# Two-block transformer kernel: the squares of three RMS norms are summed by narrower ones-products, placed later in their weight slot

## The chip, the cores and the metric

The kernel runs on one core of a Trainium2 chip. The metric is the device time in microseconds (us) of one execution; for the kernel before it is the median of three runs.

## The reference, cut to what matters

The input x has 256 tokens and 1024 features. Two "hybrid" layers (conv, mLSTM, gated linear attention, sparse attention) come first, then one block of the form

```python
h = h + 0.5 * swiglu(rmsnorm_2(h, ffn1_norm), ...)     # feed-forward part 1
n = rmsnorm_2(h, mix_norm)                             # the mixer
h = h + merged(attention(n @ w_in), gmlp(n @ w_in), gates(n)) @ w_out
h = h + 0.5 * swiglu(rmsnorm_2(h, ffn2_norm), ...)     # feed-forward part 2
return rmsnorm_2(h, final_norm)
```

where `rmsnorm(x, g) = x * rsqrt(mean(x*x, axis=-1) + 1e-6) * g`, the mean going over the 1024 features of one token. Everything is in float32.

## The kernel before, in words

**Layout.** Activations are kept transposed: `x` is 128 partitions by 8 feature tiles (`KT`) by 256 tokens (`T`). So the sum of squares over the features of a token is a sum over 8 tiles and then over 128 partitions, and the second sum is a product with a matrix of ones on TensorE.

**Weights.** They stream through the kernel as "slots" of 128 x 1024 floats. SyncE fetches slot after slot into a ring of five buffers (`raw`); ScalarE writes each slot's rounded high part into `ring` (`split`, L538), GpSimd in two halves (L415), or VectorE for some slots (L1073), writes the remainder as the low part. A slot is multiplied in 24 TensorE instructions: for each of 8 feature tiles, high weight by high x, low weight by high x, high weight by low x (`PARTS`, `tile_product`, L1803).

**The norm at the start of a part.** The norm's factor is per token, so it can be applied to the product instead of to x. The parts start with the gain applied to x (`early`, L555, and `early_lo`, L1083), multiply at once, and multiply the result by the factor when it is evacuated. The factor comes about like this. ScalarE squares x in four pieces of two tiles (`squares`, L544; the first goes to PSUM bank 3). VectorE adds the four pieces in three additions of 512 columns (`add_squares`, L1090), so that two tiles of 256 tokens side by side are left in `sqs[:, 0:512]`. TensorE multiplies each of the two with the 128 x 128 ones and accumulates both into `ps[4][:, 0:256]` (`sum_squares`, L1790). These two products have operands of plain float32 and show as four passes in the trace. VectorE scales to a mean (L1066), ScalarE takes the inverse root as exp(-0.5 ln) (L516, L517), VectorE refines it once (L1102 to L1106) and the factor is ready in `rms`.

**Where it stands in TensorE's order.** `first_two` (L1852) multiplies the part's first two slots, 48 instructions. Then `around_squares` (L1810) does the third slot: 12 instructions for the feature tiles 0 to 3, the sum of the squares, 12 instructions for the tiles 4 to 7. The part's fourth slot follows. After it TensorE needs PSUM banks again that the first slots filled: in a feed-forward part it waits for `ffn_t` (L2272), which VectorE sets when it has multiplied the first gate's result with the factor (L1542); in the mixer it waits in `m_bank_free(4)` (L2354) for `early`, set by VectorE's `early_result(0)` (two instructions of L1693).

**The five calls.** `around_squares(bank, slot, n)` is called with n = 0 and 1 for the two hybrid layers, 2 for feed-forward part 1 (starting near 586 us), 3 for the mixer (767 us), 4 for feed-forward part 2 (926 us). The final norm uses code of its own.

**Orders written out by hand.** Each engine's list is fixed in the source. Around the change VectorE's is: `early_lo`, `add_squares`, then for n = 4 the split of a weight slot (`split(FFN2_AT - 1)`, L1742, recorded at L1073), then `factor`. For n = 2 and n = 3 `factor` follows at once. ScalarE's is: `early`, `squares`, two weight splits (one for n = 4), the load of a function table (L511), a weight split, `factor`. A `step(...)` on VectorE makes the engine wait for the end of its own instruction before the next.

Of the kernel before, what the change touches and what calls it, by code (L numbers as in the profile page):

```python
# [24 lines left out]
ALU = mybir.AluOpType  # L25
# [3 lines left out]
P = 128  # L29
D = 1024  # L30
T = 256
KT = D // P
LAYERS = 2
# [106 lines left out]
GELU_A, GELU_B = 0.044715, 0.7978845608028654  # L140
N_UPDATES = 4
FINAL = LAYERS + 3
FINAL_AT = (LAYERS + 1) * (KT // 2)


# [14 lines left out]
def build(nc, d, out):  # L160
    ctx = ExitStack()
    with ctx:
# [3 lines left out]
        def sem(name):  # L166
            return ctx.enter_context(nc.semaphore(name))
# [50 lines left out]
        sqs = y[:, 8:16, :].rearrange("p a t -> p (a t)")  # L218
# [17 lines left out]
        def branch(k, part):  # L236

            return ys[:, k, part, :] if k < 4 else xs[:, k - 4, part, :]
# [18 lines left out]
        ps = [ctx.enter_context(nc.psum_tensor(f"ps{b}", [P, 512], F32)) for b in range(8)]  # L257
# [15 lines left out]
        ones = const[:, C_ONE:C_ONE + P]  # L273
# [11 lines left out]
        S = {n: sem(n) for n in names}  # L285
# [27 lines left out]
        def _(sp):  # L313
# [72 lines left out]
            for k in (0, 2, 6, 4):  # L386
                if k == 6:
                    sp.wait_ge(S["last_f"], 1)
                else:
                    sp.wait_ge(S["x_f"], FINAL_AT + k // 2 + 1)  # L390
                sp.dma_start(out[:, k:k + 2, :], xn[:, k:k + 2, :]).then_inc(S["stored"], 16)
# [660 lines left out]
        def _(dve):  # L1052
            step = Steps(dve, S["dve_steps"])
            tt, ts, stt = dve.tensor_tensor, dve.tensor_scalar, dve.scalar_tensor_tensor
# [10 lines left out]
            def mean_square(dst, src, n, done):  # L1065
                ts(dst, src, 1.0 / n, EPS, ALU.mult, ALU.add).then_inc(done, 1)  # L1066
# [19 lines left out]
            def add_squares(n):  # L1086

                for b in range(1, 4):
                    dve.wait_ge(S["sq"], n * 4 + b + 1)
                    ins = tt(ps[3][:, :] if b < 3 else sqs[:, 0:512], ps[3][:, :], sqs[:, b * 512:(b + 1) * 512],  # L1090
                             ALU.add)
                    if b < 3:
                        step(ins)
                ins.then_inc(S["sq_sum"], 1)

            def factor(n, copy=False):
# [58 lines left out]
            early_lo(0, par, V_G, True, range(4, KT))  # L1155
            split(-RING + 1)
            add_squares(0)
            split(-RING + 3)
            dve.wait_ge(S["const_in"], 16)
            dve.wait_ge(S["par_in"], 16)  # L1160

            for it in range(LAYERS):
# [315 lines left out]
                first = {50: [(ml_denominator, 2)], 52: [(ml_denominator, 3)], 65: [(ml_pair, 1)]}  # L1478
# [53 lines left out]
                update_x(it, it * LAYER_SLOTS + LAYER_SLOTS, 1.0)  # L1532
                early_lo(it + 1, par, V_G)
                add_squares(it + 1)
                split(base + LAYER_SLOTS - 1)


            def ffn(at, n, h_done, y_done, last):
# [55 lines left out]
                if not last:  # L1594
                    update_x(n, at + FFN_SLOTS, 0.25)
                    early_lo(n + 1, par2, U_MIX)
                    add_squares(n + 1)
                    for p in range(at + FFN_SLOTS - 2, at + FFN_SLOTS):
                        split(p)
# [145 lines left out]
            def end_update(a, b):  # L1745

                dve.wait_ge(S["end_out"], a // 2 + 1)
                dst = flat(x[:, a:b, :])
                stt(dst, ps[4 + a // 2][:, a % 2 * T:a % 2 * T + (b - a) * T], 0.25, dst, ALU.mult, ALU.add)\
                    .then_inc(S["end_x"], 1)  # L1750
# [14 lines left out]
            end_update(7, 8)  # L1765
            dve.wait_ge(S["ssq"], FINAL + 1)
            mean_square(var[:, 0:2], ps[4][:, 0:2], D, S["end_var"])
# [12 lines left out]
        def _(pe):  # L1780
            mm = pe.matmul

            def sum_squares(n):

                if n == 0:
                    pe.wait_ge(S["bias_sb"], 1)
                    pe.wait_ge(S["const_in"], 16)
                pe.wait_ge(S["sq_sum"], n + 1)
                for c in range(2):
                    last = mm(ps[4][:, 0:T], ones, sqs[:, c * T:(c + 1) * T], start=(c == 0), stop=(c == 1))  # L1790
                last.then_inc(S["ssq"], 1)

            PARTS = ((0, 0), (1, 0), (0, 1))
# [1 line left out]
            def tile_product(bank, half, slot, rhs, ks=range(KT), at=0, ready=None, freed=False, first=True, final=True):  # L1795

                order = [(k, w, x) for k in ks for w, x in PARTS]
                if ready:
                    order = [(k, w, 0) for k in ks for w in (0, 1)] + [(k, 0, 1) for k in ks]
                for i, (k, wp, xp) in enumerate(order):  # L1800
                    if ready and wp == 0:
                        ready(k, xp)
                    last = mm(ps[bank][:, half * T:(half + 1) * T],  # L1803
                              ring[:, slot % RING, wp, (at + k) * P:(at + k + 1) * P], rhs(k, xp),
                              start=(first and i == 0), stop=(final and i == len(order) - 1))
                    if freed and (wp, xp) == PARTS[-1] and k < KT - 1:
                        last.then_inc(S["xs_free"], 1)
                return last

            def around_squares(bank, slot, n):  # L1810

                tile_product(bank, 0, slot, xs_part, range(KT // 2), final=False)
                sum_squares(n)
                tile_product(bank, 0, slot, xs_part, range(KT // 2, KT), first=False).then_inc(S["slots_used"], 1)

            def opening():

# [127 lines left out]
            for it in range(LAYERS):  # L1945
# [242 lines left out]
                for p in range(IN_SLOTS):  # L2188
# [14 lines left out]
                    else:  # L2203
                        r = done[0]
                        if r == 2:
                            arrived(p)
                            around_squares(2, base + p, it)
                        elif r > 1:
                            bank_free(r)
                            if r == R_MQ:  # L2210
                                pe.wait_ge(S["q_fac"], it + 1)
                            arrived(p)
                            tile_product(r % 4, 0, base + p, xs_part, freed=(r == EARLY - 1)).then_inc(S["slots_used"], 1)
# [46 lines left out]
            def ffn(at, n, h_done, y_done, last=False):  # L2260
# [3 lines left out]
                first_two((0, at), (1, at + 1), xs_part, early_ready(n))  # L2264
                here(at + 2)
                around_squares(2, at + 2, n)
                here(at + 3)
                tile_product(3, 0, at + 3, xs_part).then_inc(S["slots_used"], 1)
# [92 lines left out]
            for p in range(MIX_IN_SLOTS + GATE_SLOTS):  # L2361
                slot = MIX_AT + p
                if 8 <= p < 16:
                    r, q = 8 + (p - 8) // 4 * 2, p % 4
                    if q == 0:
                        m_bank_free(r)
                        m_bank_free(r + 1)
                    here(slot)
                    if r == M_EARLY:
                        pe.wait_ge(S["x_hi"], LAYERS * KT + 2 * q + 2)  # L2370
                        pe.wait_ge(S["x_lo"], LAYERS * KT + 2 * q + 2)
                    value_slot((r % 4, r % 4 + 1), slot, q)
                else:
                    r = m_results_at(p)[0]
                    if r == 2:
                        here(slot)
                        around_squares(2, slot, 3)
                    elif r > 1:
                        m_bank_free(r)
                        here(slot)  # L2380
                        tile_product(r % 4, 0, slot, xs_part,
                                     freed=(r == M_EARLY - 1 or r == 31)).then_inc(S["slots_used"], 1)
                    if r == 1:
                        here(MIX_AT)
                        here(MIX_AT + 1)
                        first_two((0, MIX_AT), (1, MIX_AT + 1), xs_part, early_ready(3))
                for job, *which in jobs2.get(p, ()):
                    job(*which)
            for n in range(KT):

                slot = BRANCH_AT + n
# [5 lines left out]
                for g in range(2):  # L2397
                    last = tile_product(n % 4, g, slot, lambda k, part: branch(4 * g + k, part), range(4), at=4 * g,
                                        ready=(lambda k, part: pe.wait_ge(
                                            S["b_lo" if part else "b_hi"], 4 * g + k + 1)) if n == 0 else None)  # L2400
# [28 lines left out]
            for b in (5, 6):  # L2429
                for c in range(2):  # L2430
                    last = pe.transpose(ps[b][:, c * P:(c + 1) * P], rms[:, 512 + c:513 + c].broadcast_to((P, P)), ident)
# [129 lines left out]
```

## Time and profile before

| | |
|---|---|
| median of 3 runs | 1119.93 us (1119.34 to 1123.88) |
| the profiled execution's own time | 1119.74 us |
| its span, first to last instruction | 1118.0 us |
| mean granted TensorE clock | 0.997 of full speed |
| TensorE matmul busy | 1107.0 us (99%) |
| VectorE / ScalarE / GpSimd busy | 65% / 59% / 65% |
| DMA | 199.49 MB, mean 178 GB/s |

The time of an execution is 1.74 us longer than its span; what lies outside of the span is not seen in the trace. Durations in the trace are those of single instructions. TensorE's are pipelined: a product is started about every 0.11 us though each is listed with 0.28 us, so costs on TensorE are read as distances between starts.

### The profile page before, as it was taken

The page shows a single profiled execution, that of the slowest core. Times are in us where ns is not written, and L with a number is a line of the kernel's source. Part 1 is how long each engine was busy: PE and PEld are TensorE (multiplying, and loading weights), DVE is VectorE, ACT ScalarE, POOL GpSimd, SP SyncE. Part 2 cuts the span into 40 slices and gives each one's busy share as a digit, 9 for nine tenths or more (in the row PEclk, how much of TensorE's full clock was granted, in tenths as well). Part 3 has the DMA queues.
Part 4 walks back from the last instruction along what each step waited for, and adds up shares of the span by engine and source line. Part 5 has one row for each costly group of instructions (what it writes and reads, how often), then busy time and mean ns, then how long its engine had stood idle before and what let it go on. Part 6 is the DMA issues. An engine that isn't in the chain of part 4 may idle for free.

```text
span 1118.0 us, 22260 instructions
## 1 busy us (share of the span) xinstructions
PE 1107.0 (99%) x8920; PEld 1058.1 (95%) x8920; DVE 723.5 (65%) x1277; ACT 662.0 (59%) x1098; POOL 726.1 (65%) x573
## 2 busy tenths in 40 slices
PE   8999999999999999999999999999999999999997
PEld 7788999999988899899999999999899999999997
DVE  6986645576599675365848655556769567655554
ACT  7676854575577677346647444446567447544444
POOL 5787797568488868765865555445865674544442
PEclk9999999999999999999999999999999999999998
DMA  9654354546565534545666666664643655766650
GB/s 330 197 180 133 114 185 152 174 156 223 171 187 172 161 122 149 183 148 162 207 205 202 224 199 194 190 190 150 214 147 131 208 192 167 225 191 189 192 186 38
DMA packets 63895, 199.49 MB, mean 178 GB/s; under 512 B 6992, under 2 KB 17968, under 8 KB 63792
## 3 DMA queue, kind: packets, MB, share of 16 engines
q1 hardware_dynamic: 61920, 194.99, 54.4%
q10 hardware_dynamic: 1872, 3.08, 0.8%
q8 instruction: 71, 1.16, 0.4%
q14 instruction: 32, 0.26, 0.1%
HBM read 196.21 MB, written 1.84 MB: 177 GB/s over the span
## 4 chain that ended last, share of the span: by engine, by line
PE 91%; DVE 3%; ACT 3%; DMA 2%; issue 1%; SPq 0%; POOL 0%; POOLq 0%; ACTq 0%; DVEq 0%
PE ps L1803 49%; PE ps L1901 19%; PE ps L1879 12%; PE ps L2063 2%; DMA gv<-in_w 1%; PE ps L1852 1%; PE ps L2240 1%; ACT ring L538 1%; PE ps L2160 1%; PE ps L2137 1%; DMA const<-in_const 1%; PE ps L2098 1%; ACT xs L555 1%; PE ps L2037 0%; DVE score L1232 0%
## 5 line engine op out<-in xcount | busy, mean ns | idle before, releaser
L415 POOL TENSOR_TENSOR ring<-raw,ring 128x512 fp32r<-128x512 f32 x506 | 688.2, 1366 | 363.8 <-ACT ring L538 343.0
L1803 PE MATMUL ps<-xs,ring 128*128 128x256 f32 x4992 | 592.9, 278 | 0.3 <-DVE mq L1111 0.2
L1803 PEld LDWEIGHTS ps<-xs,ring 128*128 128x128 f32 x4992 | 578.1, 188 | 3.5 <-issue 1.3
L538 ACT ACTIVATE ring<-raw 128x1024 fp32r<-128x1024 f32 x360 | 379.3, 1057 | 217.0 <-PE ps L1803 119.9
L1901 PE MATMUL ps<-ys,ring 128*128 128x256 f32 x1920 | 224.4, 276 | 0.0
L1901 PEld LDWEIGHTS ps<-ys,ring 128*128 128x128 f32 x1920 | 220.7, 188 | 0.0
L1073 DVE TENSOR_TENSOR ring<-raw,ring 128x1024 fp32r<-128x1024 f32 x107 | 145.4, 1359 | 69.3 <-ACT ring L538 68.8
L1879 PE MATMUL ps<-ring,xs 128*128 128x512 f32 x672 | 164.5, 397 | 0.0
L1879 PEld LDWEIGHTS ps<-ring,xs 128*128 128x128 f32 x672 | 123.7, 188 | 26.9 <-issue 1.3
L1391 DVE SCALAR_TENSOR_TENSOR ca<-ps,par,ca 128x253 f32<-128x253 f32 (+2 forms) x96 | 45.9, 478 | 33.4 <-ACT ca L621 32.0
L1547 DVE SCALAR_TENSOR_TENSOR ca<-ps,rms 128x256 f32<-128x256 f32 x44 | 18.6, 422 | 48.7 <-PE ps L1803 48.7
L1542 DVE SCALAR_TENSOR_TENSOR ex<-ps,rms 128x256 f32<-128x256 f32 x44 | 18.6, 423 | 45.1 <-PE ps L1803 44.9
L1135 DVE TENSOR_TENSOR ys<-y,ys 128x256 fp32r<-128x256 f32 x32 | 30.8, 967 | 16.7 <-ACT ys L787 16.7
L882 ACT ACTIVATE ys<-ca 128x256 fp32r<-128x256 f32 x44 | 18.4, 418 | 34.8 <-DVE ca L1556 34.8
L1135 DVE TENSOR_TENSOR ys<-ca,ys 128x256 fp32r<-128x256 f32 x44 | 30.4, 691 | 11.0 <-ACT ys L882 11.0
L621 ACT ACTIVATE ca<-ps,par 128x256 f32<-128x256 f32 x32 | 18.0, 561 | 23.9 <-PE ps L1803 23.9
L1552 DVE TENSOR_TENSOR ca<-ca,ex 128x256 f32<-128x256 f32 x44 | 30.8, 700 | 1.5
L638 ACT ACTIVATE ex<-ps 128x256 f32<-128x256 f32 x32 | 12.2, 382 | 30.8 <-PE ps L1803 30.7
L555 ACT ACTIVATE xs<-x,par 128x256 fp32r<-128x256 f32 x40 | 16.7, 497 | 12.8 <-DVE x L1145 9.6
L1556 DVE SCALAR_TENSOR_TENSOR ca<-ex,ca 128x256 f32<-128x256 f32 x44 | 22.2, 506 | 1.4
L1852 PE MATMUL ps<-xs,ring 128*128 128x256 f32 x192 | 22.4, 276 | 0.0
L1852 PEld LDWEIGHTS ps<-xs,ring 128*128 128x128 f32 x192 | 22.1, 188 | 0.0
(300 smaller groups left out, 1047.1 us busy)
## 6 DMA issues: line engine op xcount, KB each, us to landing
raw<-in_w SPq DMA_DIRECT2D x362, 512.0 KB, 3.6
y<-bias_rows SPq DMA_DIRECT2D x6, 256.0 KB, 4.4
gv<-in_w SPq DMA_DIRECT2D x2, 512.0 KB, 7.9
out_y<-y SPq DMA_DIRECT2D x4, 256.0 KB, 2.3
const<-in_const SPq DMA_DIRECT2D x1, 896.0 KB, 6.0
bias_rows<-lg ACTq DMA_DIRECT2D x1, 768.0 KB, 6.8
x<-in_x ACTq DMA_DIRECT2D x1, 512.0 KB, 4.4
x<-in_x SPq DMA_DIRECT2D x1, 512.0 KB, 6.6
```

Source lines behind the costliest of these rows:

```text
L415: last = pool.tensor_tensor(ring[:, g % RING, 1, part], raw[:, g % RAW, part], ring[:, g % RING, 0, part].bitcast(F32), ALU.subtract)
L538: act.activation(ring[:, g % RING, 0, :], raw[:, g % RAW, :], ACT.Copy).then_inc(S["hi"], 1)
L555: act.activation(xs[:, k, 0, :], x[:, k, :], ACT.Identity, scale=g[:, col + k:col + k + 1])\
L1073: tt(ring[:, g % RING, 1, :], raw[:, g % RAW, :], ring[:, g % RING, 0, :].bitcast(F32), ALU.subtract).then_inc(lo[g % RAW], 1)
L1135: tt(ys[:, at, 1, :], src, ys[:, at, 0, :].bitcast(F32), ALU.subtract).then_inc(S["y_lo"], 1)
L1391: ins = stt(dst[:, late:T], bank[:, 0:T - late], w[:, j:j + 1], dst[:, late:T], ALU.mult, ALU.add)
L1552: step(tt(ca[:, f % 2, :], ca[:, f % 2, :], ex[:, 2 + f % 2, :], ALU.mult))
L1803: last = mm(ps[bank][:, half * T:(half + 1) * T], ring[:, slot % RING, wp, (at + k) * P:(at + k + 1) * P], rhs(k, xp), start=(first and i ...
L1852: return mm(ps[bank][:, 0:T], ring[:, slot % RING, wp, k * P:(k + 1) * P], rhs(k, xp), start=start, stop=stop)
L1879: last = mm(ps[banks[tt]][:, :].rearrange("p (j c) -> p j c", j=4), xs[:, 2 * q + k, xp, tt * P:(tt + 1) * P], w, start=(q == 0 and k == 0 ...
L1901: ins = mm(ps[4 + n // 2][:, n % 2 * T:(n % 2 + 1) * T], ring[:, slot % RING, wp, n * P:(n + 1) * P], ys[:, at, xp, :], start=(first and n ...
L2063: last = mm(second(ps[6 + e][:, (2 * tt + pr) * P:(2 * tt + pr + 1) * P]), kk[rows, keys], second(qq[rows, queries]), start=True, stop=True)
```

## The change

Every part with n >= 2 (the two feed-forward parts and the mixer; the constant `FOLDED` is `LAYERS`, 2) gets three edits. VectorE adds the two tiles that are left to one of 256 columns, after waiting for the end of the addition before. TensorE multiplies that one tile with the ones, in two products of 128 columns, each writing its own half of `ps[4][:, 0:256]` and accumulating nothing. And the sum stands after 18 of the 24 instructions of its slot (feature tiles 0 to 5) instead of after 12. The hybrid layers (n = 0 and 1) stay as they were.

```diff
+FOLDED = LAYERS
...
             def add_squares(n):
...
                     ins = tt(ps[3][:, :] if b < 3 else sqs[:, 0:512], ps[3][:, :], sqs[:, b * 512:(b + 1) * 512],
                              ALU.add)
-                    if b < 3:
+                    if b < 3 or n >= FOLDED:
                         step(ins)
+                if n >= FOLDED:
+                    ins = tt(sqs[:, 0:T], sqs[:, 0:T], sqs[:, T:2 * T], ALU.add)
                 ins.then_inc(S["sq_sum"], 1)
...
                 for c in range(2):
-                    last = mm(ps[4][:, 0:T], ones, sqs[:, c * T:(c + 1) * T], start=(c == 0), stop=(c == 1))
+                    if n >= FOLDED:
+                        last = mm(ps[4][:, c * P:(c + 1) * P], ones, sqs[:, c * P:(c + 1) * P], start=True, stop=True)
+                    else:
+                        last = mm(ps[4][:, 0:T], ones, sqs[:, c * T:(c + 1) * T], start=(c == 0), stop=(c == 1))
                 last.then_inc(S["ssq"], 1)
...
             def around_squares(bank, slot, n):
-                tile_product(bank, 0, slot, xs_part, range(KT // 2), final=False)
+                ahead = 6 if n >= FOLDED else 4
+                tile_product(bank, 0, slot, xs_part, range(ahead), final=False)
                 sum_squares(n)
-                tile_product(bank, 0, slot, xs_part, range(KT // 2, KT), first=False).then_inc(S["slots_used"], 1)
+                tile_product(bank, 0, slot, xs_part, range(ahead, KT), first=False).then_inc(S["slots_used"], 1)
```

## Rows read from the trace of the kernel before

**Rows 1.** The page: busy time, granted clock in 40 slices, the chain's shares.
```profile
PE 1107.0 (99%) x8920; PEld 1058.1 (95%) x8920; DVE 723.5 (65%) x1277; ACT 662.0 (59%) x1098; POOL 726.1 (65%) x573
...
PEclk9999999999999999999999999999999999999998
...
PE 91%; DVE 3%; ACT 3%; DMA 2%; issue 1%; SPq 0%; POOL 0%; POOLq 0%; ACTq 0%; DVEq 0%
```

**Rows 2.** Timeline of feed-forward 1's start, weight loads: start us, us, engine line op.
```profile
594.79 0.73 PEld L1790 LDWEIGHTS ps<-y,const 128*128 128x128 f32 x4
595.55 4.28 PEld L1803 LDWEIGHTS ps<-xs,ring 128*128 128x128 f32 x36
```

**Rows 3.** The same timeline: VectorE, matmuls and ScalarE.
```profile
593.66 0.69 DVE L1090 TENSOR_TENSOR y<-ps,y 128x512 f32<-128x512 f32 x1
...
594.90 1.02 PE L1790 MATMUL ps<-y,const 128*128 128x256 f32 x4
...
595.59 1.06 ACT L538 ACTIVATE ring<-raw 128x1024 fp32r<-128x1024 f32 x1
595.97 0.43 DVE L1066 TENSOR_SCALAR ps<-ps 128x256 f32<-128x256 f32 x1 [1.61 <-PE ps L1790]
...
596.56 0.36 ACT L516 ACTIVATE rms<-ps 128x256 f32<-128x256 f32 x1
...
598.80 0.42 DVE L1542 SCALAR_TENSOR_TENSOR ex<-ps,rms 128x256 f32<-128x256 f32 x1
```

**Rows 4.** Timeline of the mixer's attention, float32 products of 128 and 256 columns.
```profile
794.90 0.38 PE L2306 MATMUL ps<-dqk,mq 128*128 128x128 f32 x2
795.12 0.60 PE L2307 MATMUL ps<-dqk,mq 128*128 128x256 f32 x2
```

**Rows 5.** Source views of L1552 and L1073: duration in ns, min/median/max.
```profile
L1552 DVE TENSOR_TENSOR ca<-ca,ex x44: 424/822/1068, 599.6 to 1100.6; 128x256 f32<-128x256 f32 x44
...
L1073 DVE TENSOR_TENSOR ring<-raw,ring x107: 1209/1224/2303, 7.9 to 1093.8; 128x1024 fp32r<-128x1024 f32 x107
```

**Rows 6.** Timeline of the mixer's start: VectorE, ScalarE and the weight loads.
```profile
774.07 0.69 DVE L1090 TENSOR_TENSOR y<-ps,y 128x512 f32<-128x512 f32 x1
...
776.06 1.06 ACT L538 ACTIVATE ring<-raw 128x1024 fp32r<-128x1024 f32 x1
776.37 0.43 DVE L1066 TENSOR_SCALAR ps<-ps 128x256 f32<-128x256 f32 x1 [1.61 <-PE ps L1790]
...
777.02 0.36 ACT L516 ACTIVATE rms<-ps 128x256 f32<-128x256 f32 x1
...
779.60 0.86 DVE L1693 SCALAR_TENSOR_TENSOR mq<-ps,rms 64x256 f32<-64x256 f32 x2
...
780.51 2.68 PEld L1803 LDWEIGHTS ps<-xs,ring 128*128 128x128 f32 x23 [0.28 <-DVE mq L1693]
```

**Rows 7.** Timeline of feed-forward 2's start: VectorE, weight loads and ScalarE.
```profile
933.47 0.69 DVE L1090 TENSOR_TENSOR y<-ps,y 128x512 f32<-128x512 f32 x1
934.08 1.22 DVE L1073 TENSOR_TENSOR ring<-raw,ring 128x1024 fp32r<-128x1024 f32 x1
...
935.20 4.28 PEld L1803 LDWEIGHTS ps<-xs,ring 128*128 128x128 f32 x36
...
935.43 2.65 POOL L415 TENSOR_TENSOR ring<-raw,ring 128x512 fp32r<-128x512 f32 x2 [6.39 <-ACT ring L538]
935.61 0.43 DVE L1066 TENSOR_SCALAR ps<-ps 128x256 f32<-128x256 f32 x1 [0.32 <-PE ps L1790]
936.08 0.38 ACT L516 ACTIVATE rms<-ps 128x256 f32<-128x256 f32 x1 [0.72 <-DVE ps L1066]
...
938.34 0.42 DVE L1542 SCALAR_TENSOR_TENSOR ex<-ps,rms 128x256 f32<-128x256 f32 x1
```

**Rows 8.** Busy time by stretch (PE, PEld, DVE, ACT, POOL, clock, DMA share, GB/s).
```profile
602.00:766.00 164.00, 164.00 (x1449) 164.00 (x1448) 94.12 (x136) 79.66 (x104) 87.25 (x70) 1.00 0.64 200
```

**Rows 9.** Waits of TensorE's weight loads from 586 to 1100 us: in total, times, longest.
```profile
PEld ps L1803 <- issue: 0.3, 2, 0.2
PEld ps L1803 <- DVE mq L1693: 0.3, 1, 0.3
```

## The prediction

> **What bounds the kernel now.** I read the page first: TensorE is busy for 99% of the span, its granted clock is at the upper level (2.4 GHz) in all slices but the last, and 91% of the chain that ended last is TensorE's [rows 1]. Then the busy time by stretch: from 602 to 766 us TensorE does not pause for anything [rows 8]. So in the parts that the change touches, a nanosecond taken off TensorE's stream is a nanosecond off the end, unless TensorE then comes too early for another engine and waits. The third view is that of the waits: from 586 us on, the only wait of the stream for another engine's result is one of 0.3 us in the mixer's start, for VectorE's L1693 (0.3 us in two places more is put down to issue) [rows 9]. That wait lies right behind the code that is changed, so the fourth view is the timeline of the three places [rows 2, 3, 6, 7].
>
> **TensorE, the products.** In feed-forward 1 the sum's first weight load starts at 594.79 and the next slot instruction's at 595.55: 0.76 us for four passes. The 36 loads behind it take 4.28 us to the end of the last, which lasts 0.19, so the last starts at 599.64; the following one starts a pitch of 0.113 later, at 599.75 [rows 2]. The pitch is that of the undisturbed stream: 164.00 us over 1448 loads, 0.1133 [rows 8]. 36 x 0.1133 is 4.08, but 599.75 - 595.55 is 4.20: the last wide pass holds up the loads behind it by another 0.12. The sum costs 0.76 + 0.12 = 0.88 us.
>
> The new form has four passes too, with 128 columns instead of 256. The trace has the same shape in the attention: two passes of L2306 (128 columns, float32) take 795.12 - 794.90 = 0.22 us from start to start, 0.11 each [rows 4]. So 4 x 0.11 = 0.44, and I take 0.02 for the tail: of the 0.12, 0.10 was the wide last pass (a pass of 0.215 against a pitch of 0.113), which is gone. New cost 0.46, gain **0.42 us per part**. Bounds: without any tail the cost is 0.44 and the gain 0.44; with the whole tail of 0.12 they are 0.56 and 0.32.
>
> The Trainium skill speaks against this gain. "TensorE: Matmul & The Clock Gate", section "Back-to-back issue gap", says that a stream of weight load and product pairs has a spacing set by both, 81 ns at 128 columns and 131 ns at 512. If a float32 pass of 256 columns is taken as 512 and one of 128 as 256, that slope would save an estimated 33 ns per pass, 0.13 us per part instead of 0.42. By it no new wait would arise, and the total would be -0.13 + 0.07 - 0.13, about -0.2. No run so far shows this very product at both widths, but the trace does not agree for its neighbours in rows 4, L2306 and L2307.
>
> **VectorE, the fold.** One addition of 128 x 256, both operands in SBUF, plus the wait for the addition before it. The nearest row is L1552, of the same shape: 0.42 at least, 0.82 in the middle, 1.07 at most [rows 5]. The gap for the wait of its own end is 0.03 us. The last addition ends at 593.66 + 0.69 = 594.35 in feed-forward 1, so the fold ends between 594.81 and 595.45. TensorE asks for it six slot instructions later than before, at 594.79 + 6 x 0.1133 = 595.47. In the mixer: 774.76, fold done by 775.22 to 775.86, asked for at about 775.87 [rows 6]. In feed-forward 2: 934.16, done by 934.62 (GpSimd is idle until 935.43, and I take the short value), asked for at 935.12 [rows 7]. The move by six instructions is what covers the fold: I cost it at nothing on TensorE. Without that cover it would hold the stream by up to about 0.7. What is queued behind TensorE's wait is the sum and then six instructions of the slot; nothing else waits there.
>
> **The factor's chain.** Everything behind the sum starts later. The sum's passes used to end at 594.90 + 1.02 = 595.92 [rows 3]. Now they start 0.68 later, at 595.58, and end after three pitches of 0.11 and one duration (0.38 - 0.11 = 0.27 in rows 4): 596.18. Shift of L1066: **+0.26 us**. Does it reach the end of the chain?
> - Feed-forward 1: ScalarE's Ln started at 596.56, right behind its weight split (595.59 + 1.06), although L1066 had ended at 596.40 [rows 3]. Now L1066 ends at 596.66 and Ln starts 0.03 later: 596.69, a shift of 0.13. The gate result (L1542) ends at 598.80 + 0.42 + 0.13 = 599.35. TensorE resumes 0.05 us after such a signal (L1693 ends at 780.46, the load starts at 780.51 [rows 6]): 599.40. TensorE arrives at 599.75 - 0.42 = 599.33. **A new wait of 0.07**; net gain 0.35.
> - Mixer: Ln started at 777.02, behind its split (776.06 + 1.06); L1066 now ends at 776.37 + 0.26 + 0.43 = 777.06 and Ln starts at 777.09, a shift of 0.07. TensorE already waited for L1693 and resumed at 780.51 [rows 6]. It now arrives 0.42 earlier and resumes at 780.58: the whole 0.42 becomes wait, the old 0.3 grows to about 0.7 or 0.8, and the part is **0.07 slower**.
> - Feed-forward 2: here the split on VectorE (L1073) stands between fold and L1066. It started at 934.08, overlapping the addition by 0.08; it now starts at 934.54 and ends at 935.76, or 935.9 if GpSimd's work from 935.43 slows it. The sum arrives at 935.61 + 0.26 = 935.87, so the split just fits. Ln waited for L1066 before (0.72 idle [rows 7]), so the full 0.26 goes through: L1542 ends at 938.76 + 0.26 = 939.02, TensorE may resume at 939.07. It arrives at 935.20 + 4.28 - 0.19 + 0.11 - 0.42 = 938.98. New wait 0.09; net gain 0.33.
>
> Behind these points TensorE's stream has no pause but those two of issue [rows 8, 9], and DMA, splits and evacuations follow it, so what is gained stays gained. The slot that VectorE splits later in feed-forward 2 is needed at 939, three us after it is ready.
>
> **Sum.** -0.35 + 0.07 - 0.33 = **-0.61 us**, 0.05%. The profiled execution took 1119.74 and would take 1119.13. The median of the runs, 1119.93, is 0.19 above it, so I forecast 1119.93 - 0.6 = **1119.3 us**. A measurement of this kernel can tell about 0.5% (5.6 us) from no change; this is a ninth of that.
>
> **Rivals.**
> - **The waits do not appear** (ScalarE and VectorE run a little ahead of my working, or there is no tail). Then both feed-forward parts keep 0.42 to 0.44 and only the mixer gives back 0.07: -0.8, 1119.1. For it: the two waits that I derive are below 0.1 us. Against: each end of them is read to 0.02. Chance 0.2.
> - **Slower: the split in feed-forward 2 comes too late.** Mechanism: the fold pushes L1073 onto GpSimd's additions, and L1066 behind it starts late. It decides from the point at which fold and split together take longer than 1.7 us (from 934.16 to 935.87). At the long values, 1.07 and 2.30 [rows 5], L1066 starts at about 937.5 instead of 935.61, TensorE resumes at 939.40 + 1.30 = 940.70, and the part loses 1.3 instead of gaining 0.33: total +1.0, about 1120.9. For it: L1073 does show 2.3 us elsewhere. Against: GpSimd is idle up to 935.4 here, and 1.22 is L1073's median. Chance 0.08.
> - **The narrow passes are not cheaper**, because a pass is bound by something other than its columns (its weight load, say), or the change does not do what it says. With passes as long as now TensorE arrives as before, the feed-forward parts have 0.33 to 0.35 of slack (599.75 against 599.40, 939.40 against 939.07) and stay as they are, and the mixer loses its 0.07: +0.1, about 1120.0. Against it are rows 4, where the spacing halves with the columns (L2306 0.11; L1790 0.76 for four with the first at 0.11, so 0.215 for each of the others [rows 2]). Chance 0.1. The page of the Trainium skill named above lies between this rival and the forecast.
> - **Something else moves by tenths to one us** either way, as other overlaps of VectorE and GpSimd fall in a shifted stream (L1552 alone ranges from 0.42 to 1.07 [rows 5]). It stays inside the range. Chance 0.06.
> - The forecast itself: chance 0.55. What is left, 0.01, is a difference above 0.5% for a reason not seen here.
>
> **Range.** The cases span 1119.1 to 1120.9. Runs of the kernel before scatter by more than the effect (1119.34 and 1119.93, and one at 1123.88), so the range has to hold the scatter of a median too: **1118.3 to 1120.9**, a little over the cases below and up to the slower rival above. It leaves out a median lifted by two high runs, and what no case names. Chances: faster by over 0.5% 0.01, within 0.5% 0.98, slower by over 0.5% 0.01.
>
> **What the changed kernel's profile would show.** Products: four passes with 0.11 us between starts, and 0.44 from the first of their weight loads to the next slot instruction's, where it was 0.76. Fold: an addition of 128 x 256 of 0.42 to 1.07 us, and no idle time of TensorE before the sum. Chain: from the end of the third addition to the start of L1066 it was 595.97 - 594.35 = 1.62 in feed-forward 1 and would be 1.88, and Ln would follow L1066's end by 0.03 in all three parts. Waits: three lines where one was, for the gate result twice (under 0.15 each) and for the mixer's first results once, 0.7 to 0.8. Wrong would be: no wait in the feed-forward parts, a wait before the sum, or a distance of 0.7 or more for the four passes. An end more than 1 us away from the forecast with these three as told would mean that the cause lies outside of the changed code.

## The result: 1.2% slower, and the profile after

| | before | after |
|---|---|---|
| median (range) | 1119.86 us (1119.34 to 1123.88, 4 runs) | 1134.01 us (1132.82 to 1136.34, 4 runs) |
| profiled execution, own time / span | 1119.74 / 1118.0 | 1132.82 / 1131.0 |
| TensorE matmul busy, granted clock | 1107.0 us, 0.997 | 1120.0 us, 0.997 |

The ratio is 1.0116, with a 95% interval of 1.0098 to 1.0133. The forecast was 1119.3 us, with a range up to 1120.9 and a chance of 0.01 for more than 0.5% slower. TensorE is busy for 13 us more, with the same 8920 matmuls at the same clock. Executions of the kernel before with a mean granted clock of 0.994 to 0.996 took 1121.0 to 1124.7 us and most of the others 1118.9 to 1120.3, so the two profiled executions, both at 0.997 and 13.1 us apart, are the cleaner pair. The busy shares show nothing: TensorE's is 99% in both. What shows the loss is the number of weight loads that pass in a fixed stretch. Here is the view of busy time by stretch for the weight loads of the kernel before, in the middle of feed-forward 1 and of feed-forward 2 (busy us, number of loads, granted clock, DMA share, GB/s):

```profile
610.00:760.00 150.00, 150.00 (x1325) 1.00 0.64 200
955.00:1105.00 150.00, 150.00 (x1325) 1.00 0.56 176
```

and the same view of the changed kernel:

```profile
610.00:760.00 150.00, 150.00 (x1275) 1.00 0.61 192
955.00:1105.00 150.00, 150.00 (x1275) 1.00 0.59 187
```

150 us hold 1325 loads before and 1275 after: 0.1132 us against 0.1176 from load to load, with no idle time in either and the clock at 1.00 in both. (A count takes in the one or two loads that reach over the ends of the stretch, which matters in the short stretches further down.) Read load by load, the two distances are 0.1133 and 0.1178. I call them the **fast pace** and the **slow pace**. Some 1580 loads follow the sum of feed-forward 1 up to the mixer's, and some 1520 that of feed-forward 2; at 0.0044 us each that is 7.0 and 6.7 us. Compared load by load, the changed kernel lies 0.43 us ahead of the kernel before up to the first changed sum (the code there is the same, and this comes from the first 60 us), 6.15 behind where the mixer's sum comes, 6.74 behind from the mixer's attention to its end, and 13.06 behind at the end. So 6.6 us are lost from feed-forward 1's sum to the mixer's, 0.6 in the rest of the mixer, 6.3 from feed-forward 2's sum on, and nothing elsewhere.

This is where it begins, in the changed kernel's timeline of feed-forward 1's start, with the weight loads, the matmuls, VectorE and ScalarE [rows 2, 3]:

```profile
595.05 0.53 PEld L1794 LDWEIGHTS ps<-y,const 128*128 128x128 f32 x4
595.16 0.60 PE L1794 MATMUL ps<-y,const 128*128 128x128 f32 x4
595.17 1.06 ACT L539 ACTIVATE ring<-raw 128x1024 fp32r<-128x1024 f32 x1
595.49 4.66 PEld L1809 LDWEIGHTS ps<-xs,ring 128*128 128x128 f32 x39
...
595.80 0.43 DVE L1067 TENSOR_SCALAR ps<-ps 128x256 f32<-128x256 f32 x1 [1.24 <-PE ps L1794]
596.27 0.38 ACT L517 ACTIVATE rms<-ps 128x256 f32<-128x256 f32 x1
...
598.52 0.43 DVE L1545 SCALAR_TENSOR_TENSOR ex<-ps,rms 128x256 f32<-128x256 f32 x1
```

The four narrow passes take 0.44 us from the first load to the next slot instruction's, as forecast. But the 39 loads behind them take 4.66 - 0.19 = 4.47 from the first start to the last, 0.1176 each. In the kernel before, read load by load, the stream is back at 0.1133 after five loads. Here the slow pace stays for 187 us. In the mixer (same four passes) the stream enters slow and leaves fast, then waits for L1696 (L1693 before) and goes on slow [rows 6]; in feed-forward 2 it enters fast and leaves slow [rows 7]:

```profile
782.05 0.53 PEld L1794 LDWEIGHTS ps<-y,const 128*128 128x128 f32 x4
...
782.50 3.49 PEld L1809 LDWEIGHTS ps<-xs,ring 128*128 128x128 f32 x30
...
786.78 0.54 PEld L1809 LDWEIGHTS ps<-xs,ring 128*128 128x128 f32 x4 [0.79 <-DVE mq L1696]
...
941.86 0.52 PEld L1794 LDWEIGHTS ps<-y,const 128*128 128x128 f32 x4
...
942.30 4.79 PEld L1809 LDWEIGHTS ps<-xs,ring 128*128 128x128 f32 x40
```

From the first start to the last that is (3.49 - 0.19) / 29 = 0.114 in the mixer, which is fast, and (4.79 - 0.19) / 39 = 0.118 in feed-forward 2, which is slow. The waits of TensorE's weight loads from 586 us on, in the changed kernel [rows 9]:

```profile
PEld ps L1809 <- DVE mq L1696: 0.8, 1, 0.8
PEld ps L1809 <- issue: 0.3, 2, 0.2
```

The two waits that I had put into the feed-forward parts are not there: at the slow pace TensorE arrives later.

And the slow pace was to be seen in the kernel before. I had read its stretch from 602 us and taken that for "the undisturbed stream". Its timeline shows a stretch near the start, and one behind a piece of attention (821.82) next to a fast one (817.99):

```profile
22.05 5.01 PEld L1803 LDWEIGHTS ps<-xs,ring 128*128 128x128 f32 x42
```

```profile
817.99 2.81 PEld L1803 LDWEIGHTS ps<-xs,ring 128*128 128x128 f32 x24
...
821.82 2.78 PEld L1803 LDWEIGHTS ps<-xs,ring 128*128 128x128 f32 x23
```

(5.01 - 0.19) / 41 is 0.1176. In the second pair, 24 loads take 2.81 and 23 take almost as long. The durations of single loads differ too. These are min/median/max in ns from 610 to 760 us, first before and then after; one load in three is at 192 there, and the slow stretch at 821.82 in the kernel before has the 192 as well:

```profile
L1803 PEld LDWEIGHTS ps<-xs,ring x893: 187/188/188, 609.8 to 759.9; 128*128 128x128 f32 x179
L1809 PEld LDWEIGHTS ps<-xs,ring x844: 187/188/192, 609.9 to 757.2; 128*128 128x128 f32 x169
```

### The profile page after: what moved, and what is told of

The parts are those of the page before. It is cut to its first block, busy times and chain, and to the rows that moved or that the text cites. A ratio compares the mean times of both kernels' runs of the same rounds, so it can differ in the third digit from the quotient of the medians.

```text
span 1131.0 us, 22263 instructions
## 1 busy us (share of the span) xinstructions
PE 1120.0 (99%) x8920; PEld 1071.4 (95%) x8920; DVE 720.7 (64%) x1280; ACT 662.3 (59%) x1098; POOL 726.8 (64%) x573
## 4 chain that ended last, share of the span: by engine, by line
PE 92%; DVE 3%; ACT 2%; issue 1%; DMA 1%; SPq 0%; POOLq 0%; ACTq 0%; DVEq 0%
PE ps L1809 50%; PE ps L1908 19%; PE ps L1886 11%; PE ps L2070 2%; PE ps L1859 1%; DMA gv<-in_w 1%; PE ps L2247 1%; PE ps L2167 1%; PE ps L2144 1%; PE ps L2105 1%; PE ps L2044 0%; DVE score L1235 0%; PE ps L2131 0%; PE ps L2147 0%; PE ps L2168 0%
## 5 line engine op out<-in xcount | busy, mean ns | idle before, releaser
L1809 PE MATMUL ps<-xs,ring 128*128 128x256 f32 x4992 | 601.7, 280 | 0.7 <-DVE mq L1696 0.6
L1809 PEld LDWEIGHTS ps<-xs,ring 128*128 128x128 f32 x4992 | 586.8, 188 | 3.7 <-issue 1.3
L1908 PE MATMUL ps<-ys,ring 128*128 128x256 f32 x1920 | 228.8, 279 | 0.0
L1908 PEld LDWEIGHTS ps<-ys,ring 128*128 128x128 f32 x1920 | 225.0, 188 | 0.0
L1074 DVE TENSOR_TENSOR ring<-raw,ring 128x1024 fp32r<-128x1024 f32 x107 | 144.6, 1351 | 70.9 <-ACT ring L539 70.0
L1859 PE MATMUL ps<-xs,ring 128*128 128x256 f32 x192 | 22.6, 277 | 0.0
L1859 PEld LDWEIGHTS ps<-xs,ring 128*128 128x128 f32 x192 | 22.3, 188 | 0.0
```

Source lines behind the costliest of these rows:

```text
L1074: tt(ring[:, g % RING, 1, :], raw[:, g % RAW, :], ring[:, g % RING, 0, :].bitcast(F32), ALU.subtract).then_inc(lo[g % RAW], 1)
L1809: last = mm(ps[bank][:, half * T:(half + 1) * T], ring[:, slot % RING, wp, (at + k) * P:(at + k + 1) * P], rhs(k, xp), start=(first and i ...
L1859: return mm(ps[bank][:, 0:T], ring[:, slot % RING, wp, k * P:(k + 1) * P], rhs(k, xp), start=start, stop=stop)
L1908: ins = mm(ps[4 + n // 2][:, n % 2 * T:(n % 2 + 1) * T], ring[:, slot % RING, wp, n * P:(n + 1) * P], ys[:, at, xp, :], start=(first and n ...
```

## The experiments

The theory to be tested had several forms. **W**: the width of the passes in front sets the pace. **P**: the place in the slot does. **F**: the fold on VectorE does. **C**: the stream has two steady paces, and every interruption (a block of other passes, or a wait) can put it on either. Each edit is given against the changed kernel unless said otherwise. Where the sum is repeated, the product's result is the same; where an extra product is added, its result is not used.

**1. The move alone.** Fold and narrow products undone, `ahead = 6` kept:

```diff
-                    if b < 3 or n >= FOLDED:
+                    if b < 3:
                         step(ins)
-                if n >= FOLDED:
-                    ins = tt(sqs[:, 0:T], sqs[:, 0:T], sqs[:, T:2 * T], ALU.add)
...
-                    if n >= FOLDED:
-                        last = mm(ps[4][:, c * P:(c + 1) * P], ones, sqs[:, c * P:(c + 1) * P], start=True, stop=True)
-                    else:
-                        last = mm(ps[4][:, 0:T], ones, sqs[:, c * T:(c + 1) * T], start=(c == 0), stop=(c == 1))
+                    last = mm(ps[4][:, 0:T], ones, sqs[:, c * T:(c + 1) * T], start=(c == 0), stop=(c == 1))
```

> The change's move alone: no fold, the old two products of 256 columns (four wide passes), placed after 18 instructions of the slot instead of 12. In the changed kernel the weight loads of both feed-forward parts follow each other at 0.1178 us from the sum on, where they did at 0.1133 before; some 3100 instructions times 0.0044 are the 13 us. Theory W (the width of the passes in front of the stream sets its pace): with wide passes the pace is 0.1133 in both feed-forward parts, time 1120 to 1121 (the chain of the factor is 0.7 later, so waits of up to 0.4 per part). Theory P (the place in the slot sets it): pace 0.1178, time 1133 to 1134.

Measured: 1126.76 us (1126.54 to 1127.34, 4 runs), ratio 1.0061 (1.0046 to 1.0076). Neither number that was expected. The busy time of the weight loads by stretch shows why; the first two stretches lie on either side of 940.0, the last two are those of the tables above:

```profile
937.00:940.00 3.00, 3.00 (x28) 1.00 0.58 188
940.40:945.40 5.00, 5.00 (x44) 1.00 0.48 179
955.00:1105.00 150.00, 150.00 (x1275) 1.00 0.56 178
610.00:760.00 150.00, 150.00 (x1325) 1.00 0.63 200
```

Feed-forward 1 is fast, feed-forward 2 slow (44 loads in 5 us, where experiment 5 has 46 at the fast pace). And in feed-forward 2 the pace behind the sum is fast (load by load 0.1133); behind the load at 940.03 the next one comes only 0.213 later, a wait of 0.1 for the gate result (L1543 ends at 940.18), since the factor's chain is 0.7 later; from there it is slow. In feed-forward 1 the same gap, 0.213 at 599.75, leaves it fast. So a wait can switch the pace as well, and need not.

**2. One wide product over the folded tile.**

```diff
-                for c in range(2):
-                    if n >= FOLDED:
-                        last = mm(ps[4][:, c * P:(c + 1) * P], ones, sqs[:, c * P:(c + 1) * P], start=True, stop=True)
-                    else:
-                        last = mm(ps[4][:, 0:T], ones, sqs[:, c * T:(c + 1) * T], start=(c == 0), stop=(c == 1))
+                for c in range(1 if n >= FOLDED else 2):
+                    last = mm(ps[4][:, 0:T], ones, sqs[:, c * T:(c + 1) * T], start=(c == 0),
+                              stop=(c == 1 or n >= FOLDED))
```

> The changed kernel with one product of 256 columns (two wide passes) over the folded tile instead of two of 128 (four narrow passes); fold and move stay. Theory W: pace 0.1133 in both feed-forward parts, and the sum costs 0.11 + 0.22 + 0.12 = 0.45 us, so 1119.2 to 1119.8, level with the kernel before or 0.5 faster. Theory P, or a theory F that lays the slow pace on the fold on VectorE: 0.1178, time 1133 to 1134. Theory C (any change of the number of cycles spent at this point can put the stream on either pace): either, but clearly one of the two.

Measured: 1133.46 us, ratio 1.0123 (1.0104 to 1.0142). No narrow pass is left, and both feed-forward parts are slow, from the first loads behind the sum. That refutes W.

```profile
610.00:760.00 150.00, 150.00 (x1275) 1.00 0.62 194
955.00:1105.00 150.00, 150.00 (x1275) 1.00 0.59 187
```

**3. Narrow, but not moved** (`ahead = 4`).

> The changed kernel without the move: fold and four narrow passes, but after 12 instructions of the slot. TensorE then has to wait for the fold, 0.1 to 0.7 us in each part. Theory W: pace 0.1178 in both feed-forward parts whatever the place, time 1133 to 1135. Theory P: 0.1133, time 1120 to 1121. Theory C: either one, and a part can differ from the other, since the wait ends at no fixed cycle.

Measured: 1125.90 us (1120.66 to 1130.34, 10 runs), ratio 1.0051 (1.0035 to 1.0068). The ten runs fall into groups: one at 1120.7, seven from 1125.5 to 1126.2, two at 1129.4 and 1130.3. The last two have mean clocks of 0.995 and 0.994, which by the kernel before is enough to lift 1126 by that much; that leaves no and one slow part, by time alone, since only one execution was profiled. In the profiled one feed-forward 1 is slow and feed-forward 2 fast:

```profile
594.98 0.52 PEld L1794 LDWEIGHTS ps<-y,const 128*128 128x128 f32 x4 [0.18 <-DVE y L1096]
```

```profile
610.00:760.00 150.00, 150.00 (x1275) 1.00 0.61 193
955.00:1105.00 150.00, 150.00 (x1325) 1.00 0.59 186
```

Here TensorE waits for the fold in front of the passes (0.18 in this row). In both feed-forward parts the first of them comes 0.365 after the load before it, and the four passes are the same; one part leaves them slow and the other fast. So with the wait the outcome is no longer the same in the two parts, nor, by the groups, in all executions. P is out: in experiment 1 both parts ran fast right behind a sum at the changed kernel's place, and here a part is slow at the place of the kernel before.

**4. A wide product behind the narrow ones.**

```diff
                 last.then_inc(S["ssq"], 1)
+                if n >= FOLDED:
+                    mm(ps[5][:, 0:T], ones, sqs[:, 0:T], start=True, stop=True)
```

> The changed kernel with one more product of ones and 256 columns (two wide passes, its result unused, into bank 5) behind the narrow ones; it costs some 0.4 us on TensorE per part. Theory W, if only the last passes count: pace 0.1133 in both feed-forward parts, 1119.8 to 1120.5. If any narrow pass does it, or theories P and F: 0.1178, 1134. Theory C: either.

Measured: 1119.93 us (1119.20 to 1122.71, 10 runs), ratio 1.0001 (0.9991 to 1.0011): 14 us less than the changed kernel, though the longer block takes 0.44 us more of TensorE's time per part. Everything that the change does is in this kernel, the place of the sum too. Loads in the two stretches:

```profile
610.00:760.00 150.00, 150.00 (x1325) 1.00 0.63 199
955.00:1105.00 150.00, 150.00 (x1326) 1.00 0.56 176
```

**5. Moved by three instructions instead of six** (against the first experiment: `ahead = 5`).

> As the kernel with the move alone (no fold, four wide passes), but with the sum after 15 slot instructions instead of 18. There both feed-forward parts ran at 0.1133 right behind the sum; feed-forward 2 went over to 0.1178 only behind a wait of 0.1 us for the first gate result, 30 instructions later. With 15 the chain is 0.34 late instead of 0.68 and TensorE, with 0.48 and 0.59 of slack, does not wait. Theory C (the stream has two steady paces, and each interruption, a block of other passes or a wait, puts it on one or the other): no interruption besides the sum, so 0.1133 in both parts and 1119.9 to 1120.3. Theory P (a later place of the sum makes the stream slow): feed-forward 2 at 0.1178 again, 1126 to 1127.

Measured: 1120.64 us (1119.19 to 1124.50, 10 runs), ratio 1.0005 (0.9990 to 1.0020). There is no wait for the gate result, and both parts are fast. Together with the first experiment this puts the loss of the move alone on the wait that it brings; that the place itself (18 instructions) does not do it is seen in experiment 1, which is fast up to the wait.

**6. Fold, and the wide product issued twice** (four wide passes as before the change, `ahead = 5`):

```diff
-                        last = mm(ps[4][:, c * P:(c + 1) * P], ones, sqs[:, c * P:(c + 1) * P], start=True, stop=True)
+                        last = mm(ps[4][:, 0:T], ones, sqs[:, 0:T], start=True, stop=True)
```

> The fold on VectorE, then the product of 256 columns over the folded tile issued twice (four wide passes, as in the kernel before; the second writes the same values again), after 15 slot instructions, so that TensorE waits neither for the fold nor for the gate result. Theory C: the same passes behind the same stream as in the kernel before give the same pace, 0.1133 in both feed-forward parts, 1119.8 to 1120.3. Theory F (the fold, or the data it leaves, makes the stream slow): 0.1178, 1133 to 1134.

Measured: 1119.49 us (1119.42 to 1123.10, 10 runs), ratio 0.9990 (0.9977 to 1.0002). F is out. It is the lowest median of all, but its interval holds 1.

**7. The narrow products issued twice** (`for c in (0, 1, 0, 1)` for n >= 2; eight narrow passes).

> The changed kernel with its two narrow products issued twice (eight narrow passes instead of four). Theory C: the pace right behind the sum may be either one, and the changed kernel shows both for four narrow passes (from 0.1133 to 0.1178 in the feed-forward parts, from 0.1178 to 0.1133 in the mixer); I expect the same pace right behind the sum in both feed-forward parts, and at most one change behind a later wait: 1119.5 to 1120.5 if fast, 1126 to 1134 if not. Theory N (narrow passes always leave the slow pace): 0.1178 behind the sum in all three parts, 1133 to 1134.

Measured: 1135.67 us, ratio 1.0131 (1.0103 to 1.0159). Slow behind the sum in both feed-forward parts; in the mixer from slow to fast, as with four. Theory N, which wanted slow in all three, fails at the mixer.

**8. The kernel before with a wait put in.**

```diff
                     if f == 2:
-                        pe.wait_ge(S["ffn_t"], h_done + 1)
+                        pe.wait_ge(S["ffn_e"], h_done + 1)
```

> The kernel before with one edit: ahead of the fifth slot of each feed-forward part TensorE waits for ScalarE's first tanh instead of VectorE's first gate result, which comes some 0.35 us after TensorE arrives. The sum is as it was. Theory C: a wait can change the pace as the passes can, so each feed-forward part may come out at 0.1178 behind the wait (7 us each): 1120.5 if none, 1127 if one, 1134 if both do, and it may differ between executions. Theory S (only the sum's passes count): 0.1133 everywhere and 1120.5.

Measured: 1121.75 us (1120.12 to 1129.09, 10 runs), ratio 1.0018 (0.9997 to 1.0038). In the profiled execution (1120.27) both parts stay fast behind waits that put 0.460 and 0.360 between two loads. Two other runs took 1126.6 and 1126.7, at mean clocks of 0.998 and 0.997, and one 1129.1 at 0.995. That is where one slow part would put them, but they have no trace. Inconclusive by itself; it fits a wait that rarely switches.

**9. A reset five slots later**: the changed kernel, with four wide passes in the running stream of each feed-forward part.

```diff
                     here(slot)
+                    if f == 3:
+                        for c in range(2):
+                            mm(ps[2][:, 0:T], ones, sqs[:, 0:T], start=True, stop=True)
                     tile_product(2 * (f % 2), 0, slot, xs_part).then_inc(S["slots_used"], 1)
```

> The changed kernel, and in each feed-forward part, five slots behind the sum (ahead of the gate product of tile 3), two more products of ones and 256 columns (four wide passes, 0.9 us, results overwritten at once). Theory C: the slow pace is a state of TensorE's stream that lasts until the stream is interrupted, and nothing else in the part is slow. A block of four wide passes can end it: then 0.1178 up to some 611 us and 0.1133 behind in both parts, 1134.0 - 2 x 6.3 + 2 x 0.9 = about 1123. If such a block does not end the slow state (so far it was only seen to leave a fast stream fast), the pace stays and the time is about 1136. Theory M (the slow pace comes from something that the changed start leaves in place for the whole part, such as memory traffic in another rhythm): 1136 as well, with 0.1178 on both sides of the block.

Measured: 1121.88 us (1120.95 to 1123.62, 10 runs), ratio 1.0009 (0.9995 to 1.0022), where 1123 was expected for C and 1136 for M. The weight loads by stretch, before and behind the block at 607.96 and the one at 949.05:

```profile
597.00:607.00 10.00, 10.00 (x86) 1.00 0.69 216
611.00:621.00 10.00, 10.00 (x90) 1.00 0.74 231
938.00:948.00 10.00, 10.00 (x87) 1.00 0.61 186
952.00:962.00 10.00, 10.00 (x90) 1.00 0.75 250
```

The pace changes at the block, so M is out, and the slow pace is nearly the whole loss. Start, fold, narrow passes and move are those of the changed kernel; 0.9 us of useless work per part ends the slow pace, and 12 of the 14 us are back.

**10. Six wide passes** (experiment 6 with the product issued three times).

> The fold, and the product of 256 columns issued three times (six wide passes), after 15 slot instructions. So far two wide passes left the slow pace and four the fast one. Theory T (the total that the block keeps the stream busy must be long enough for the fast pace, or at least four wide passes be there): 0.1133, 1120.0 to 1120.8. Theory C without such a rule: either pace, the same in both feed-forward parts; slow would be 1134.

Measured: 1136.05 us (2 runs), ratio 1.0129 (1.0096 to 1.0162); slow in both parts. Theory T is out: longer is not safer.

**11. Two wide passes, then four narrow** (experiment 4 in the other order).

```diff
+                if n >= FOLDED:
+                    mm(ps[4][:, 0:T], ones, sqs[:, 0:T], start=True, stop=True)
                 for c in range(2):
```

> The same six passes as the run with a wide product behind the narrow ones (fast), in the other order: two wide passes, then four narrow ones, after 18 slot instructions. Theory L (what counts is what stands last, narrow leaving the slow pace): 0.1178 behind the sum in both feed-forward parts, about 1134. Theory T (the count or the total length): 0.1133, 1119.5 to 1121.

Measured: 1126.61 us median of five runs that lie far apart: 1120.0, 1120.3 and 1126.6, all at a mean clock of 0.998, then 1130.0 at 0.995 and 1138.3 at 0.994. By their times these may be no, one and two slow parts; only the one at 1126.6 has a trace. Behind the sum the pace is fast in all three parts, so L is out too. Then TensorE waits for the gate result (the chain is 0.4 later than in the changed kernel), 0.196 and 0.199 from load to load; feed-forward 1 stays fast, feed-forward 2 turns slow:

```profile
610.00:760.00 150.00, 150.00 (x1325) 1.00 0.64 201
955.00:1105.00 150.00, 150.00 (x1275) 1.00 0.58 178
```

**12. One wide product after 17 instructions instead of 18** (against experiment 2, inside a feature tile).

> The kernel with one wide product (two wide passes, slow in both parts), with the sum after 17 instructions of the slot instead of 18, so not between two feature tiles but between a tile's second and third product. The stream's starts repeat in a pattern of three (113, 113, 114 ns), as the products of a tile do. Theory Q (the place within that pattern of three decides): the fast pace may come out, 1119.2 to 1119.8. Theory L or T (the passes decide, not the place): 0.1178 as before and 1133 to 1134.

Measured: 1133.05 us (2 runs), ratio 1.0102 (1.0070 to 1.0134), slow in both parts. The place is not what decides.

**All blocks together.** Read load by load in the profiled executions of this study and of the kernel before, at the sums of the three parts and at the resets of experiment 9, with the number of blocks seen. The two blocks of experiment 3 with a wait right in front are left out. Each kernel has one profiled execution, and blocks of one kernel repeat the same code, so the counts are not as many independent trials.

| passes in the block | stream was fast | stream was slow |
|---|---|---|
| 2 wide | slow (4 of 4) | slow (2 of 2) |
| 4 wide | fast (15 of 15) | fast (2 of 2) |
| 6 wide | slow (2 of 2) | fast (1 of 1) |
| 4 narrow | slow (5 of 5) | fast (2 of 2) |
| 8 narrow | slow (2 of 2) | fast (1 of 1) |
| 4 narrow, 2 wide | fast (3 of 3) | |
| 2 wide, 4 narrow | fast (3 of 3) | |

For a given block and a given pace in front, the pace behind was always the same. Two wide passes led to the slow pace from either side and four wide passes to the fast one; six wide, four narrow and eight narrow exchanged the two. The sums of the two hybrid layers, four wide passes in all 14 traces, are not in the table and fit it: all 28 leave the fast pace behind them, 20 of them from the fast and 8 from the slow. I know no rule that gives these outcomes from the passes: not the width, the count, the length of the block or what stands last.

## Why the prediction was wrong, point by point

- **The step that failed** is the one that carried 0.1133 us across the change: "Behind these points TensorE's stream has no pause but those two of issue", and from that, "what is gained stays gained"; with it goes "The pitch is that of the undisturbed stream: 164.00 us over 1448 loads, 0.1133". There is no pause, and yet the loads come 0.0044 us further apart. The interruption in front of a long stream, here the block of four narrow passes, decides at which of two paces it runs. The term was taken as zero, and it is 7.0 + 6.7 us in the two feed-forward parts and 0.4 in the mixer.
- **The products: right.** 0.44 us from the first load to the next slot instruction's, passes 0.11 apart [rows 4]. The gain shows on the spot: over feed-forward 1's sum the changed kernel's lead grows from 0.43 to 0.86, and over the mixer's its lag shrinks from 6.15 to 5.76, with six loads at the slow pace in between (forecast: 0.42). The rate at which the Trainium skill's page "TensorE: Matmul & The Clock Gate", section "Back-to-back issue gap", lets the spacing grow with the columns does not agree: four passes fell from 0.76 to 0.44, 0.32 before the tail, where its slope made 0.13.
- **The fold: right.** It took 0.60, 0.58 and 0.42 us, inside the bounds of [rows 5], and the weight loads do not wait for it in the changed kernel. The move covers it; without the move the wait is there (experiment 3, 0.18).
- **The chain: right.** From the end of the third addition (593.24 + 0.69) to L1067 it is 1.87 in feed-forward 1, where 1.88 was forecast. In feed-forward 2 the split on VectorE (L1074) ran 1.22 and was done before L1067 began.
- **The waits: half right.** The mixer's grew from 0.3 to 0.8, as forecast. The two in the feed-forward parts were worked out for the fast pace, at which TensorE never ran there; that they would be missing had been named as a sign of being wrong.
- **The rivals.** None of them had a pace that switches. "Something else moves by tenths to one us" had the right place in the list, and a size that was too small by more than ten times (one us at most, against 13), because I took the spread of VectorE's durations for it and not that of TensorE's own distances. The slow pace stood in the trace of the kernel before, and a query of the distance for each stretch would have found it.
- **What remains open** is the rule by which a block leads to one pace or the other, and what in TensorE the two paces are. At the slow pace one load in three lasts 192 or 193 ns, at the fast one none lasts more than 188; what that says of the cause is open too. Whether a wait switches the pace could not be steered: the same distance of 0.213 left one part fast and one slow. Whether other data or other buffers in the same block would change its outcome was not tried.

## What to carry to other kernels

Where one engine is busy for 99% of the span, its distance from start to start times the number of instructions is the time, and a change of 4% in that distance outweighs the removal of single instructions: here 13.7 us in two parts, against a gain of 0.42 us in each. So read the distance by stretch, count of instructions over time, before and after an edit, above all behind the point where the edit breaks a long uniform stream; and if it has two values in the trace before, a forecast needs a case for the other one. If an edit leaves the stream slow, another harmless block at the same point or later can bring it back, and it has to be tried on the chip. Here two more wide passes were worth 14 us, and a block of four wide passes was followed by the fast pace every time that it was seen (45 blocks, ten of them from the slow pace).

## What the runs showed of the hardware that was not expected

- A stream of weight load and matmul pairs with 256 columns runs at 0.1133 or at 0.1178 us per pair, at the same granted clock of 1.00 and with no idle time, and in the feed-forward parts kept the pace that it had for 170 to 190 us, until something interrupted it (1325 or 1275 loads in 150 us). At the slow pace one weight load in three took 192 or 193 ns; at the fast one none took more than 188.
- Blocks of two to eight float32 passes switched it, by the table above. A wait of about 0.1 us switched it in two of four places (experiments 1 and 11).
- The executions of one kernel can differ by the 6 to 7 us of one part when a wait stands in front: 1120.0 and 1120.3 against 1126.6 in experiment 11, all at a mean clock of 0.998. That it is the pace is read from the times; of each such kernel only one execution has a trace.
